# The beginning of a fused two-block transformer kernel: loads asked for as earlier ones land, rotary angles and one slab's subtraction on GpSimd, parameters turned in the value projection

## What is computed

```python
def rms_norm(x, g):
    return x * lax.rsqrt(jnp.mean(x * x, axis=-1, keepdims=True) + EPS_RMS) * g

def dilated_attention_mixer(x, positions, w_qkv, w_o):
    qkv = (x @ w_qkv).reshape(B, S, 3, GH, HEAD_DIM)       # 1024 -> 9216
    inv_freq = ROPE_THETA ** (-jnp.arange(0, ROT_DIM, 2) / ROT_DIM)
    ang = positions[..., None] * inv_freq
    cos, sin = jnp.cos(ang), jnp.sin(ang)
    q, k = rope_partial(qkv[:, :, 0], cos, sin), rope_partial(qkv[:, :, 1], cos, sin)
    ...

for i in range(DEPTH):
    a = rms_norm(h, mix_norm_pre[i])
    h = h + rms_norm(mixer(a), mix_norm_post[i])
    h = h + rms_norm(conv_ffn(rms_norm(h, ffn_norm_pre[i])), ffn_norm_post[i])
```

## Time and profile before

| | us |
|---|---|
| median of 3 runs | 2149.15 (2147.18 to 2150.51) |
| profiled execution: span, first to last instruction | 2143.4 |
| the median over that span | 5.7 |
| PE busy in the span | 2108.3 (98%) |
| DVE, ACT, POOL busy | 1477.1, 1017.9, 481.6 |
| PE begins tile (1, 0) of qk | 34.76 after the start |

### The profile page before, as it was taken

How to read it: one execution, slowest core, us unless ns; L and a number is a source line. 1 busy time by engine, 2 the same in 40 slices (tenths; PEclk the granted TensorE clock), 3 DMA queues, 4 the chain that set the end, 5 groups by cost and what they waited for, 6 DMA issues and landing times.

```text
span 2143.4 us, 43268 instructions
## 1 busy us (share of the span) xinstructions
PE 2108.3 (98%) x16240; PEld 1928.0 (90%) x16240; DVE 1477.1 (69%) x2517; ACT 1017.9 (47%) x1377; POOL 481.6 (22%) x518
## 2 busy tenths in 40 slices
PE   8999999999999999999999999999999999999999
PEld 7997779989999888799889987799889998779998
DVE  7884778857688667688678846788565546586553
ACT  4335765544455443555443346655453334364332
POOL 3220005510135314044212200054113300201320
PEclk9999999999999999999999999999999999999999
DMA  6555235565645644245645553255645556305554
GB/s 189 187 178 185 89 125 177 193 201 181 206 144 189 208 155 148 69 158 193 205 160 182 190 179 117 83 183 190 204 150 173 171 182 187 99 21 177 185 180 145
DMA packets 300950, 350.37 MB, mean 163 GB/s; under 512 B 7604, under 2 KB 255990, under 8 KB 300854
## 3 DMA queue, kind: packets, MB, share of 16 engines
q1 hardware_dynamic: 296358, 344.75, 49.4%
q10 hardware_dynamic: 4112, 4.07, 0.6%
q0 software_dynamic: 384, 0.24, 0.0%
HBM read 346.35 MB, written 2.68 MB: 163 GB/s over the span
## 4 chain that ended last, share of the span: by engine, by line
PE 90%; DVE 4%; ACT 4%; issue 1%; ACTq 0%; DVEq 0%
PE ps L2312 26%; PE ps L2314 26%; PE ps L2313 26%; PE ps L2741 2%; DVE w_lo L1693 1%; ACT w_hi L1263 1%; PE ps L2449 1%; PE ps L2444 1%; PE ps L2445 1%; ACT prob L566 1%; PE ps L2678 1%; PE ps L2381 1%; PE ps L2691 1%; PE ps L2324 1%; PE ps L2290 0%
## 5 line engine op out<-in xcount | busy, mean ns | idle before, releaser
L1693 DVE TENSOR_TENSOR w_lo<-raw,w_hi 128x2048 fp32r<-128x2048 f32 (+3 forms) x310 | 694.0, 2239 | 452.9 <-ACT w_hi L1263 452.7
L2312 PE MATMUL ps<-a_hi,w_hi 128*128 128x256 f32 (+1 forms) x3200 | 906.2, 283 | 6.2 <-DVE w_lo L1702 2.7
L2314 PE MATMUL ps<-a_hi,w_lo 128*128 128x256 f32 (+1 forms) x3200 | 903.3, 282 | 0.0
L2313 PE MATMUL ps<-a_lo,w_hi 128*128 128x256 f32 (+1 forms) x3200 | 903.1, 282 | 0.0
L1263 ACT CAST w_hi<-raw 128x2048 fp32r<-128x2048 f32 (+3 forms) x318 | 587.4, 1847 | 542.2 <-PE ps L2314 528.5
L2312 PEld LDWEIGHTS ps<-a_hi,w_hi 128*128 128x128 f32 x3200 | 604.8, 189 | 12.8 <-issue 5.8
L2314 PEld LDWEIGHTS ps<-a_hi,w_lo 128*128 128x128 f32 x3200 | 605.5, 189 | 0.0
L2313 PEld LDWEIGHTS ps<-a_lo,w_hi 128*128 128x128 f32 x3200 | 602.5, 188 | 0.4 <-issue 0.2
L2217 POOL TENSOR_TENSOR hs<-sg,cv 128x256 f32<-128x256 f32 x88 | 65.5, 744 | 642.6 <-DVE cv L2054 642.6
L2224 POOL CAST hid_hi<-hs 128x256 f32 (+3 forms) x132 | 137.8, 1044 | 297.0 <-DVE hs L2100 282.7
L2312 PE MATMUL ps<-w_hi,hid_hi 128*128 128x512 f32 x480 | 189.5, 395 | 2.3 <-DVE w_lo L1689 1.2
(11 more groups left out here) (359 smaller groups left out, 2552.5 us busy)
## 6 DMA issues: line engine op xcount, KB each, us to landing
raw<-in_ffn_w_in_dram SPq DMA_DIRECT2D x88, 1024.0 KB, 5.1
raw<-in_attn_w_qkv_dram SPq DMA_DIRECT2D x71, 1024.0 KB, 5.1
raw<-in_ffn_w_out_dram SPq DMA_DIRECT2D x32, 1024.0 KB, 5.0
raw<-in_ffn_w_gate_dram SPq DMA_DIRECT2D x22, 1024.0 KB, 5.3
raw<-in_ffn_w_up_dram SPq DMA_DIRECT2D x22, 1024.0 KB, 5.3
raw<-in_ffn_w_down_dram SPq DMA_DIRECT2D x16, 896.0 KB, 4.8
raw<-in_sc_w_in_dram SPq DMA_DIRECT2D x12, 1024.0 KB, 5.1
raw<-in_ffn_w_out_dram SPq DMA_DIRECT2D x16, 768.0 KB, 4.5
```

Source lines behind the costliest of these rows:

```text
L1693: dve.tensor_tensor(o, src, hi.bitcast(F32), ALU.subtract).then_inc(lo_ready, 1)
L2312: pe.matmul(o, wh, xh, start=start, stop=False)
L2313: pe.matmul(o, wh, xl, start=False, stop=False)
L2314: return pe.matmul(o, wl, xh, start=False, stop=stop)
```

## The change

- SP asks for x in two halves of its columns, the first ahead of all but the identity. It waits for that half to land before it asks for the second and for the rest of slab 0, and for the first half of slab 0 before it asks for slab 1. The parameter rows are split in three shares; SP asks for one before slab 2 and one between slabs 2 and 3, and only then for lambda, mask and the small constants.
- The rotary angles are computed by POOL in 15 steps (3 of the former fused DVE steps become two each), each waiting for the one before; ACT's sines wait for the last. Then POOL subtracts slab 2 (`lo_by_pool`), and then it asks for the last share of parameter rows.
- DVE splits slab 0's first half after `a_lo` 0 and 1, its second after 2 and 3; the four moments, the rms factors and the tables follow slab 1. After the four `rope_tab` it waits for POOL's slab and counts it in `lo_ready` with a memset.
- ACT casts slab 0's halves after `a_hi` 1 and 3, casts slab 2 before the sines, and leaves the copies of parameters and mask to "v".
- PE: 8 warm-up matmuls instead of 30, 8 more before the first real one; the row is spread after tile 3, and the parameters are turned at the start of "v", lambda's sum in its iteration 0.

```diff
@@ load_params
-                    if n % 2 == share:
+                    if n % 3 == share:
@@ sync
-            sp.dma_start(first[:, 0:4, :], w0[:, 0:4, :]).then_inc(raw_first, 16)
-            for t in range(2):
-                sp.dma_start(h_tok[:, t, :], xv[:, t, :]).then_inc(x_landed, 16)
+            sp.dma_start(h_tok[:, :, 0:512], xv[:, :, 0:512]).then_inc(x_first, 16)
+            sp.dma_start(first[:, 0:4, :], w0[:, 0:4, :]).then_inc(raw_first, 16)
+            sp.wait_ge(x_first, 16)
+            sp.dma_start(h_tok[:, :, 512:], xv[:, :, 512:]).then_inc(x_landed, 16)
             sp.dma_start(first[:, 4:, :], w0[:, 4:, :]).then_inc(raw_landed[0], 16)
+            sp.wait_ge(raw_first, 16)
             sp.dma_start(slab_view(raw, streams[0], 1, 1), streams[0].src(0, 1)).then_inc(raw_landed[1], 16)
...
             load_params(sp, 0, par_landed)
...
                 if ph.s0 == 0:
-                    lo = 1
+                    load(1, 0)
+                    load_params(sp, 1, par_landed)
+                    load(1, 1)
+                    first_constants()
+                    lo = 2
@@ scalar
-                act.wait_ge(arg_ready, 2)
+                act.wait_ge(arg_ready, 15)
...
                         if not n and k == 1:
+                            act.wait_ge(raw_first, 16)
+                            act.copy(first[0][:, 0:4, :], first[1][:, 0:4, :]).then_inc(hi_half, 1)
+                        if not n and k == 3:
                             act.wait_ge(raw_landed[0], 16)
                             act.copy(first[0][:, 4:, :], first[1][:, 4:, :]).then_inc(hi_ready, 1)
...
+                        load_table(act, ACT.Sin)
+                        split_hi(ph.dense, 1, 0)
                         first_tables()
...
-                    if not ph.dense.off:
-                        split_hi(ph.dense, 1, 0)
-                        first_params()
...
-                    if not ph.dense.off:
-                        first_casts()
...
+                        if i == 0 and not ph.no:
+                            first_params()
+                            first_casts()
@@ vector
                             if k == 1:
+                                first_low(hi_half, 1, 0)
+                            if k == 3:
                                 first_low(hi_ready, 1, 1)
-                            if 2 <= k <= 4:
-                                first_rest((PI_A, PI_B, PI_C)[k - 2])
-                            if k > 4:
-                                moments(k - 5)
-                        first_edges()
                         split_low_half(ph.dense, 0)
                         split_low_half(ph.dense, 1)
...
-                        moments(3)
+                        for c in range(4):
+                            moments(c)
                         mean_squares()
+                        factors()
                         first_tables()
-                        factors()
...
-                        split_lo(ph.dense, 1, 0)
+                        if n:
+                            split_lo(ph.dense, 1, 0)
...
                     link(last)
+                    if ph.s0 == 0:
+                        dve.wait_ge(lo_by_pool, 1)
+                        dve.memset(mark[:, 2:3], 0.0).then_inc(lo_ready, 1)
@@ gpsimd
-            load_params(pool, 1, par_landed_pool)
+            def angle(ins):
+                steps[0] += 1
+                ins.then_inc(arg_ready, 1)
+                pool.wait_ge(arg_ready, steps[0])
+            pool.wait_ge(pos_landed, 32)
+            angle(pool.tensor_copy(trig[0][:], pos_i[:]))
+            angle(pool.tensor_scalar(trig[1][:], trig[0][:], freq[:, 0:1], None, ALU.mult))
...
+            pool.wait_ge(hi_ready, 3)
+            pool.tensor_tensor(w_lo[0][:], raw[0][:], w_hi[0][:].bitcast(F32), ALU.subtract).then_inc(lo_by_pool, 1)
+            load_params(pool, 2, par_landed_pool)
@@ tensor
-            warm_up(30)
+            warm_up(8)
...
+                            warm_up(8)
                             pe.wait_ge(lo_half, 1)
...
                     tile(ph, None, 2)
-                    if not n:
-                        turn_params()
-                    if tok:
+                    if tok and n:
                         spread_row()
                     tile(ph, None, 3)
+                    if not n:
+                        spread_row()
...
                     if not ph.no:
-                        pe.wait_ge(par_ready, 3)
-                        pe.wait_ge(lam_exp, 1)
+                        turn_params()
```

More of the change, by code:

```diff
@@ L451, in build @@
         par_landed, par_landed_pool = sem("par_landed"), sem("par_landed_pool")
[L452 removed]
+        pos_landed, lam_landed, lo_by_pool = sem("pos_landed"), sem("lam_landed"), sem("lo_by_pool")
         consts_cast, par_turned, par_ready = sem("consts_cast"), sem("par_turned"), sem("par_ready")
@@ L1246, in first_params @@
                 act.wait_ge(lam_done, 1)
-                act.activation(lexp, ps[:, 6, 0:2], ACT.Exp).then_inc(lam_exp, 1)
+                act.activation(lexp, ps[:, 7, 0:2], ACT.Exp).then_inc(lam_exp, 1)
             def first_casts():
@@ L1285, in _ @@
             first = [slab_view(t, streams[0], 0, 0) for t in (w_hi, raw)]
-            act.wait_ge(raw_first, 16)
-            act.copy(first[0][:, 0:4, :], first[1][:, 0:4, :]).then_inc(hi_half, 1)
             act.wait_ge(par_ready, 1)
@@ L1628, in _ @@
             dve.memset(mark[:, 26:27], 0.0).then_inc(silu_ready, 2)
-            def first_angles():
-                dve.wait_ge(pos_landed, 32)
-                link(dve.tensor_copy(trig[0][:], pos_i[:]))
-                link(dve.tensor_scalar(trig[1][:], trig[0][:], freq[:, 0:1], None, ALU.mult))
-                link(dve.tensor_scalar(trig[0][:], trig[1][:], 1.0 / TWO_PI, ROUND, ALU.mult, ALU.add))
-                link(dve.tensor_scalar(trig[0][:], trig[0][:], ROUND, None, ALU.subtract))
-            def first_rest(part):
-                link(dve.scalar_tensor_tensor(out=trig[1][:], in0=trig[0][:], scalar=-part, in1=trig[1][:],
-                                              op0=ALU.mult, op1=ALU.add))
-            def first_edges():
-                edge = 3.1415925
-                link(dve.tensor_scalar(trig[3][:], trig[1][:], math.pi / 2, None, ALU.add))
-                dve.tensor_scalar(trig[2][:], trig[1][:], edge, -edge, ALU.min, ALU.max).then_inc(arg_ready, 1)
-                link(dve.tensor_scalar(trig[0][:], trig[3][:], math.pi, -TWO_PI, ALU.is_gt, ALU.mult))
-                link(dve.tensor_tensor(trig[3][:], trig[3][:], trig[0][:], ALU.add))
-                dve.tensor_scalar(trig[3][:], trig[3][:], edge, -edge, ALU.min, ALU.max).then_inc(arg_ready, 1)
             def first_tables():
@@ L1886, in _ @@
                         split_ahead(ph, i, False)
+                    if not ph.no:
+                        first_small()
                     split_lo(ph, ph.n - 1, 1)
@@ L2204, in _ @@
         def _(pool):
-            load_params(pool, 1, par_landed_pool)
+            steps = [0]
+            def angle(ins):
+                steps[0] += 1
+                ins.then_inc(arg_ready, 1)
+                pool.wait_ge(arg_ready, steps[0])
+            edge = 3.1415925
+            pool.wait_ge(pos_landed, 32)
+            angle(pool.tensor_copy(trig[0][:], pos_i[:]))
+            angle(pool.tensor_scalar(trig[1][:], trig[0][:], freq[:, 0:1], None, ALU.mult))
+            angle(pool.tensor_scalar(trig[0][:], trig[1][:], 1.0 / TWO_PI, ROUND, ALU.mult, ALU.add))
+            angle(pool.tensor_scalar(trig[0][:], trig[0][:], ROUND, None, ALU.subtract))
+            for part in (PI_A, PI_B, PI_C):
+                angle(pool.tensor_scalar(trig[2][:], trig[0][:], -part, None, ALU.mult))
+                angle(pool.tensor_tensor(trig[1][:], trig[2][:], trig[1][:], ALU.add))
+            angle(pool.tensor_scalar(trig[3][:], trig[1][:], math.pi / 2, None, ALU.add))
+            angle(pool.tensor_scalar(trig[2][:], trig[1][:], edge, -edge, ALU.min, ALU.max))
+            angle(pool.tensor_scalar(trig[0][:], trig[3][:], math.pi, -TWO_PI, ALU.is_gt, ALU.mult))
+            angle(pool.tensor_tensor(trig[3][:], trig[3][:], trig[0][:], ALU.add))
+            angle(pool.tensor_scalar(trig[3][:], trig[3][:], edge, -edge, ALU.min, ALU.max))
+            pool.wait_ge(hi_ready, 3)
+            pool.tensor_tensor(w_lo[0][:], raw[0][:], w_hi[0][:].bitcast(F32), ALU.subtract).then_inc(lo_by_pool, 1)
+            load_params(pool, 2, par_landed_pool)
             for ph in phases:
@@ L2305, in turn_params, with lambda_sums @@
                         mm.then_inc(par_turned, 1)
+            def lambda_sums():
                 pe.wait_ge(start_set, 3)
                 pe.wait_ge(lprod_ready, 1)
-                pe.matmul(ps[:, 6, 0:2], ones[0:HD, :], lprod, start=True, stop=True).then_inc(lam_done, 1)
```

(8 more changed lines are left out.)

40 lines of the change are left out of this document (20 added, 20 removed).

## The result

The changed kernel takes 2155.53 us (median of 8 runs), the kernel before 2148.42 beside it (8 runs): ratio 1.0026, 95% interval [1.0017, 1.0036], so slower by 3.7 to 7.7 us. One of the eight executions took 4125.51 us, at a granted clock of 1.0, for a reason that nothing here shows; the ratio leaves it out, and the median of the other seven is 2155.34. The profiled execution spans 2153.5 us. The predicted 2155.3 is met, but hardly by the way the prediction took: two of its three terms were wrong, one in its sign.

A forecast was written before the change was run, and what follows sets the result against it. It took PE, busy 98% of the span, as the bound. Tile (1, 0) +2.8, clock +2.0 and "v" +1.3 made +6.1 us: span 2143.4 to 2149.5, plus 5.7 to the median, 2155.3 us; range 2146 to 2160.

The forecast's parts named there:

- its three terms: Start of tile (1, 0) +2.8 us, clock loss +2.0, PE work moved into "v" +1.3.
- the loads: Beginning: x's half lands at about 5.5 us, PE starts at 11.3, tile 2 at 18.8, tile 3 ends at 24.5.
- The angles: POOL's rotary angles before tile (1, 0): steps of 0.92 or 0.74 us with 0.17 between, ready at 27.4 us.
- The slab: POOL's subtraction of slab 2 takes 5.3 us after the angles, so slab 2 is ready at 33.0.
- What waits: Root, `spread`, row, tables and first rope follow POOL's work; PE begins tile (1, 0) at 37.6, 2.8 us later.
- The lock: DVE's `spread` waits for POOL's whole slab subtraction over the shared SBUF ports; without that wait 2.2 us less.
- rival 1: `spread` does not wait for POOL; tile (1, 0) begins at 35.4, +3.9 us in all, 2153.1; chance 0.20.
- rival 2: POOL's one-input steps are quick, 0.4 us; tile (1, 0) at 31.7, +0.2 us in all, 2149.4; chance 0.18.
- The clock: PE idles from 24.5 to 37.6 but for the row; the slow clock afterwards costs 2.0 us, bounds 1.6 and 3.2.
- Moved into "v": Turning parameters and lambda's sum at the start of "v" costs PE +1.3 us; ACT's copies are covered by PE's tiles.
- The sum: Whole kernel: +2.8, +2.0 and +1.3 make +6.1 us, 2155.3 us, 0.28% slower; chance 0.40.

The follow-up runs named there:

- experiment 9: Changed kernel with slab 2 on DVE, an idle second operation in GpSimd's one-operation steps, and a reordered beginning: 2147.88 against 2149.24 us for the kernel before, ratio 0.9993.
- experiment 3: Changed kernel with GpSimd's subtraction of slab 2 in four instructions of 512 columns instead of one of 2048: one execution, 2152.54 us.
- experiment 7: Changed kernel with 14 idle matmuls on PE behind tile 3 and 11 behind the row: 2150.17 against 2149.24 us for the kernel before, ratio 1.0006.
- experiment 5: Changed kernel with ACT's parameter copies and constant casts in two gaps of iteration 0 of "v" instead of one piece: 2153.15 us, ratio 1.0023 to the kernel before.

## Why the number was right and the steps were not

*What bounds the kernel, the loads.* Right: fixed work on PE, and the start of tile (1, 0). PE started at 10.89 (11.3 predicted), tile 2 at 19.13 (18.8), tile 3 ended at 24.9 (24.5), and, as the text warned, none of this sets the end. x's first half landed at 7.0, not 5.5, but the warm-up covered it.

*The angles, first wrong step.* 27.4 predicted, 22.67 measured. The frequencies landed at 7.85, not 8.5. The gap between steps is 0.08 to 0.09, not 0.17: 1.2 us over 14 gaps. "The same operation and both its instances are alike" was the weak argument: the two instances were both one-operation steps, which take 0.85 to 0.93 here, while two-operation steps take 0.40 where nothing holds them (0.41 in place of 0.86 once an idle operation is added, experiment 9). The rest, 2.9 us, is 2.3 for these steps and 0.6 for shorter standstills beside DVE's work (mostly the steps of 1.71, 1.38, 0.82 and 1.94), 3.4 in all where 4.0 were set. By the Trainium skill (GPSIMD Engine Reference, Engine selection) one-input operations are roughly line-rate; the trace has that for the CAST and the two-operation form, 0.40 each, and not for the one-operation form. The 6 us for a first call (same page, Instruction dispatch) is not there: the first TENSOR_SCALAR began 0.1 us behind the CAST and took 0.93.

*The slab.* 5.3 taken, 4.55 measured, within the bounds 4.2 and 5.9.

*What waits, right mechanism, wrong place.* The lock was taken to catch `spread`, behind the root. It caught the mean squares, ahead of the root, since the angles were early: DVE reached these two tiny instructions 0.4 us after GpSimd's long one began. From the end of that one, 4.6 us to tile (1, 0) were predicted and 5.3 measured, as the root came behind it too. The term came out as -2.2 instead of +2.8 because the whole train left 5.7 us earlier. That `spread` waits, which the prediction assumed without a row, experiment 3 shows. (Where the prediction draws on the Trainium skill, SBUF — State Buffer, for `tensor_scalar`, the page has it in its section Who interferes with whom, and only as an operation that can contend; the wait itself rests on the trace.) The outcome lies between rival 1 and rival 2; rival 2's time for tile (1, 0), 31.7, was nearest, and its total, 2149.4, was 6 us too low all the same.

*The clock, right in size, by a guess.* 2.0 predicted, 2.0 measured, and experiment 7 shows the cause, PE's idling, and 1.9 us in its profile. But 2.0 was picked between two bounds for one idle time of some 13 us; what came were waits of 3.5 and 2.9.

*Moved into "v", under-sized.* 1.3 for PE's work; measured 1.1 and 0.5. The failed step is "ACT's copies in iteration 0 ... are covered by PE's tiles, since both engines are idle for much of an iteration". Idle time in an engine is no cover for a piece of 2.1 us put just ahead of the cast that is due: +1.7 us, gone with the piece in two gaps (experiment 5).

*The sum.* -2.2 + 1.9 + 1.6 + 1.7 = +3.0 us of work and waits, against +6.1. The mean spans (2152.5 over 16 runs, 2147.3 over 89) differ by 5.2. The other 2.2 fit the clock further back, in the middle of the program, and slabs that land late, which the profiles show; how much of either the change brings about no run tells. No row of before showed either, since its one profile was among its better executions: a timed run is 1.9 us longer than its span, so of the 5.7 that the prediction put between span and median 3.8 were this one execution's good fortune. The late slabs near 1095 us are in three profiles of the twelve and in that of the result; why is not settled. So the number was met by luck: an error of 5 us for tile (1, 0) was offset by terms that the prediction lacked, +1.7 for ACT's piece, +0.3 for lambda and some 2 that stay open.

## What to carry to other kernels

Before a long two-input instruction goes to GpSimd, list every small DVE instruction, down to one element a row, that falls into its length and ask who waits for it: the length is paid by the first one on the path, and cutting the instruction into four made each small one pay for a piece, for a gain of 0.5 us. When work is moved into a stage with "idle" helpers, look for the gap it fits in, by time, and never put it ahead of the cast or split that feeds the bound engine. Where PE must wait, fill the wait with idle matmuls and see whether the granted clock holds: it did for waits of 3.5 and 2.9 us, and not at 490 us. Compare a kernel's clock over many runs before one profile is taken for its usual state.

## Hardware behaviour that was not expected

- GpSimd's TENSOR_SCALAR of 128x256 f32 took 0.85 to 0.87 us with one operation and an immediate, 0.93 with a factor per row, and 0.40 to 0.41 with two operations, where DVE did not hold it up; the same step with an idle second operation took 0.41, and 0.48 with a factor per row.
- A DVE instruction of 128x1 took up to 4.2 us beside one of GpSimd.
- Around two waits of PE, 3.5 and 2.9 us with the 1.15 us row between them, the clock fell to 1.2 GHz for 6.8 or 10.3 us; behind single waits of 2.7 and 1.9 us it did so for 3.4. Near 305 us it fell for 3.4 us or 6.9 in nine of twelve profiles, where 3.8 us of small fp32 matmuls and transposes and a wait of 0.88 us stand ahead; in the one profile of the kernel before, with the same work and the same wait, it did not.
